# Where the low half of the value weights is made: from GpSimd to VectorE, between the product with the gates and its own low half

## What is computed

```python
def peer(h, w_q, sub_keys, expert_u, expert_v):
    ...
    s_fin, pos = lax.top_k(cand, PEER_TOPK)          # 8 heads x 16 of 16384 experts per token
    ids = jnp.take_along_axis(ids_cand, pos, axis=-1)
    gates = jax.nn.softmax(s_fin, axis=-1)
    ...
        a = jax.nn.gelu(jnp.einsum('cd,ckd->ck', xc, expert_u[idc]))
        return jnp.einsum('ck,ckd->cd', gc * a, expert_v[idc])
```

## Time and profile before

| | us |
|---|---|
| median of 3 runs | 1842.11 (1841.93 to 1848.57) |
| the profiled execution | 1840.62 |
| its span, first to last instruction | 1838.6 |
| TensorE busy in it | 1724.5 (94%) |
| VectorE busy | 1284.1 (70%) |
| GpSimd busy | 1151.2 (63%) |

### The profile page before, as it was taken

How to read it: one execution, slowest core, us unless ns; L and a number is a source line. 1 busy time by engine, 2 the same in 40 slices (tenths; PEclk the granted TensorE clock), 3 DMA queues, 4 the chain that set the end, 5 groups by cost and what they waited for, 6 DMA issues and landing times.

```text
span 1838.6 us, 26701 instructions
## 1 busy us (share of the span) xinstructions
PE 1724.5 (94%) x9077; PEld 1474.0 (80%) x9077; DVE 1284.1 (70%) x2106; ACT 741.6 (40%) x1105; POOL 1151.2 (63%) x701
## 2 busy tenths in 40 slices
PE   6988999999999999998399999999999999999997
PEld 5766778888788999998399999997777777777775
DVE  6678521221221499999999999618888888888887
ACT  5477632322332333332166666533333333333333
POOL 6522224444433468887377777768778888888883
PEclk9999999999999999999699999999999999999999
DMA  6211122222322358787479999989979999999993
GB/s 240 92 46 46 36 69 92 98 96 95 99 69 80 124 167 294 255 258 240 151 245 347 345 344 347 356 334 378 355 301 336 351 356 348 339 345 360 353 343 111
DMA packets 127105, 424.76 MB, mean 231 GB/s; under 512 B 13264, under 2 KB 29648, under 8 KB 124880
## 3 DMA queue, kind: packets, MB, share of 16 engines
q1 hardware_dynamic: 89904, 289.45, 45.3%
q0 software_dynamic: 36864, 134.23, 19.1%
q10 hardware_dynamic: 288, 0.54, 0.1%
HBM read 371.74 MB, written 52.43 MB: 231 GB/s over the span
## 4 chain that ended last, share of the span: by engine, by line
PE 45%; DVE 40%; ACT 6%; issue 5%; DMA 2%; DVEq 1%; SPq 0%; POOL 0%; ACTq 0%
PE both L512 14%; DVE wf L1502 12%; PE bank L523 9%; DVE both L1518 8%; PE bank L512 7%; PE bank L527 5%; DVE rows L1386 4%; ACT wT_hi L1102 3%; PE bank L805 2%; DVE cand L1369 2%; PE bank L722 2%; DVE cand L1426 2%; DVE cand L1423 1%; PE bank L822 1%; DVE topi L1375 1%
## 5 line engine op out<-in xcount | busy, mean ns | idle before, releaser
L466 POOL TENSOR_TENSOR w_lo<-raw,w_hi 128x1024 fp32r<-128x1024 f32 (+1 forms) x430 | 862.8, 2015 | 610.3 <-ACT w_hi L870 608.4
L870 ACT ACTIVATE w_hi<-raw 128x1024 fp32r<-128x1024 f32 x346 | 365.9, 1058 | 599.2 <-PE bank L527 287.5
L523 PE MATMUL bank<-hT_hi,w_hi 128*128 128x384 f32 x1024 | 348.0, 340 | 0.0
L523 PE MATMUL bank<-hT_lo,w_hi 128*128 128x384 f32 x1024 | 343.4, 335 | 0.0
L487 POOL DMA_INDIRECT rows<-stream,idx x256 | 284.8, 1112 | 60.4 <-issue 27.1
L1502 DVE TENSOR_TENSOR wf<-a_in,g_in 128x384 f32<-128x384 f32 x128 | 236.9, 1850 | 27.9 <-DMA a_in<-a_rows 26.3
L822 PE MATMUL bank<-w_hi,wT_hi 128*128 128x512 f32 x768 | 211.6, 410 | 31.1 <-ACT wT_hi L1102 29.6
L822 PEld LDWEIGHTS bank<-w_hi,wT_hi 128*128 128x128 f32 x768 | 134.7, 188 | 105.7 <-ACT wT_hi L1102 79.2
L1102 ACT ACTIVATE wT_hi<-wf 128x384 fp32r<-128x384 f32 x128 | 66.9, 523 | 370.1 <-DVE wf L1502 366.3
L527 PE MATMUL bank<-hT_hi,w_lo 128*128 128x384 f32 x1024 | 199.9, 336 | 6.3 <-POOL w_lo L466 6.3
L822 PE MATMUL bank<-w_hi,wT_lo 128*128 128x512 f32 x768 | 196.6, 391 | 0.0
(11 more groups left out here) (249 smaller groups left out, 2204.0 us busy)
## 6 DMA issues: line engine op xcount, KB each, us to landing
raw<-stream SPq DMA_DIRECT2D x346, 512.0 KB
a_rows<-abuf SPq DMA_DIRECT2D x64, 384.0 KB
g_rows<-gstage SPq DMA_DIRECT2D x32, 768.0 KB
g_in<-g_rows SPq DMA_DIRECT2D x16, 1536.0 KB
a_in<-a_rows SPq DMA_DIRECT2D x64, 384.0 KB
rows<-stream,idx POOLq DMA_INDIRECT x256
x_sb<-x SPq DMA_DIRECT2D x4, 512.0 KB, 8.7
out<-x_sb SPq DMA_DIRECT2D x4, 512.0 KB, 2.6
```

Of the source, the lines that this page charges most:

```text
L466: last = pool.tensor_tensor(w_lo[:, k % 2, cols], raw[:, k % RAW, cols], w_hi[:, k % 2, cols].bitcast(f32), ALU.subtract)
L523: pe.matmul(dst, w_hi[:, slot, k * P:(k + 1) * P], hT[low][:, k, DENSE], start=(k == 0 and low == 0), stop=False)
L870: act.activation(w_hi[:, base % 2, :], raw[:, slot, :], ACT.Copy).then_inc(hi_ready, 1)
```

## The change

In the value stage the low half of the weights is no longer made by GpSimd but by VectorE, as the second of its instructions in a step: after `wf` and ahead of `wT_lo`. It has a semaphore of its own, `value_lo_ready`, on which TensorE and the raw loads of that stage now wait. GpSimd's program in the value stage holds gathers alone, which wait only for a free slot (`dotted`, eight back). The number of matmuls, transfers and bytes stays the same.

```diff
--- before.py
+++ after.py
@@ -238,6 +238,7 @@
 
         raw_loaded = [sem(f"raw_loaded{i}") for i in range(RAW)]
         hi_ready, lo_ready, chunk_used = sem("hi_ready"), sem("lo_ready"), sem("chunk_used")
+        value_lo_ready = sem("value_lo_ready")
         proj_read = sem("proj_read")
         mem_loaded, gains_loaded, small_loaded = sem("mem_loaded"), sem("gains_loaded"), sem("small_loaded")
         x_loaded = [sem(f"x_loaded{t}") for t in range(TT)]
@@ -298,8 +299,10 @@
             a_rows = dram["a"]
             g_rows = dram["g"]
 
-            def load(n, slot, fresh=False):
-                if not fresh:
+            def load(n, slot, fresh=False, value=None):
+                if value is not None:
+                    sp.wait_ge(value_lo_ready, value)
+                elif not fresh:
                     sp.wait_ge(lo_ready, n - RAW + 1)
                 sp.dma_start(raw[:, slot, :], stream[bass.ds(n, 1), :, :].rearrange("n p c -> p (n c)")
                              ).then_inc(raw_loaded[slot], 16)
@@ -385,7 +388,8 @@
 
             for k in range(I_TAIL):
                 at = I_PLAIN + I_GATES + k
-                load(first_u + at, (first_u + at) % RAW)
+                early = first_u + at - RAW + 1 - S_EV
+                load(first_u + at, (first_u + at) % RAW, value=early if early > 0 else None)
                 if k % 2:
                     store_a(0, at // 2)
                 if k == 0:
@@ -409,7 +413,7 @@
 
             def value_step(j0, k, more=True, again=True):
                 if more:
-                    load(j0 * 2 + (nxt + k), (nxt + k) % RAW)
+                    load(j0 * 2 + (nxt + k), (nxt + k) % RAW, value=j0 * 2 + (nxt + k - RAW + 1 - S_EV))
                 if k % 2 and again:
                     reload_a(j0, k // 2 + 4)
 
@@ -490,7 +494,8 @@
 
             g = 0
             for c in range(2 * NI):
-                low(S_U + c, S_U + c)
+                if c < NI:
+                    low(S_U + c, S_U + c)
                 while g < 2 * HK and gather_after(g) <= c:
                     gather(g)
                     g += 1
@@ -833,11 +838,11 @@
                 if not final:
                     for t in range(1, TT):
                         both(t, wT_lo, w_hi)
-                    pe.wait_ge(lo_ready, n + i0 + 1)
+                    pe.wait_ge(value_lo_ready, i0 + (di + 1))
                     for t in range(1, TT):
                         last = both(t, wT_hi, w_lo)
                 else:
-                    pe.wait_ge(lo_ready, n + i0 + 1)
+                    pe.wait_ge(value_lo_ready, i0 + (di + 1))
                     for t in range(1, TT):
                         both(t, wT_lo, w_hi)
                         last = both(t, wT_hi, w_lo, stop=True)
@@ -1502,6 +1507,11 @@
                 dve.tensor_tensor(wf[:, di % 2, :].rearrange(tiles, b=BLOCKS),
                                   a_in[:, di % 8, :].rearrange(tiles, b=BLOCKS),
                                   g_in[:, di // GROUP, :, di % GROUP, :], ALU.mult).then_inc(weighted, 1)
+                dve.wait_ge(hi_ready, i0 + (S_EV + di + 1))
+                if first:
+                    dve.wait_ge(chunk_used, S_EV + di - 1)
+                dve.tensor_tensor(w_lo[:, di % 2, :], raw[:, (S_EV + di) % RAW, :], w_hi[:, di % 2, :].bitcast(f32),
+                                  ALU.subtract).then_inc(value_lo_ready, 1)
                 dve.wait_ge(weighted_hi, i0 + (di + 1))
                 dve.tensor_tensor(wT_lo[:, di % 2, :], wf[:, di % 2, :], wT_hi[:, di % 2, :].bitcast(f32),
                                   ALU.subtract).then_inc(weighted_lo, 1)
```

## The result

The changed kernel takes 1785.95 us (median of 4 runs, 1785.6 to 1787.23), the kernel before 1842.02 beside it (4 runs, 1841.87 to 1848.57). The ratio is 0.9683, 95% interval 0.9664 to 0.9701. The forecast was 1779 in a range of 1771 to 1801: the sign, the mechanism and the range held, and the time is 7 us over the forecast. It lies 1 us above the band of 1772 to 1785 that stood for DMA keeping up, within the band of the DMA rival, though what that rival says did not happen; the account behind the experiments says what lifted it.

What follows compares the result with a forecast made beforehand. VectorE, held up by GpSimd's subtraction, was taken to bound the value stage. Chunk 6 at 1264.7, 121 chunks of 4.08 (493.7), 15.0 behind, 2.0 around, 2 for late loads: 1777.4; median 1.5 higher, 1779 us, range 1771 to 1801.

Steps and rivals of the forecast that it cites:

- DMA keeping up: Value stage: DMA can carry the 388 GB/s that 4.08 us a chunk needs; 1772 to 1785 us, chance 0.62.
- the DMA rival: Value stage: DMA holds today's ratio, 378 GB/s, 4.19 us a chunk, 13 us more, 1792; band 1785 to 1800, chance 0.18.
- The room, 0.526 us a chunk: Value stage: chunks can fall from 4.606 us to TensorE's 4.08, a floor the change cannot pass.
- `wf` shortened by the overlap: VectorE, value stage: without GpSimd subtracting at the same time, `wf` falls from a mean of 1.85 us to about 0.56.
- Price of the subtraction: VectorE, value stage: the moved 1024-column subtraction takes 1.22 us, 1.14 from start to start, between 1.05 and 2.40.
- VectorE's step of 3.75: Value stage: VectorE's work per step after the change, gathered rows included, 3.75 us, under TensorE's 4.08.
- The new wait: VectorE, value stage: `w_lo` waits for ScalarE's `w_hi` in about every third step, at most 1 us; costed at nothing.
- The estimate from the 358 GB/s of the Trainium skill: Value stage: at about 358 GB/s between HBM and SBUF a chunk takes 4.43 us, the sum 42 us higher, 1821.
- the 353: Value stage: DMA rate of the stage's best whole window; as ceiling, 4.49 us a chunk, 50 us more, 1829, chance 0.05.
- The entry: Start of the value stage: DMA backlog lets chunk 6 start between 1262.8 and 1266.6, early gathers delaying it; middle 1264.7 taken.
- late raw loads: After the value stage's entry: some raw loads come late while the DMA backlog goes down; 2 us added.
- Chunk 0 starts at 1237.23 and that stays: Start of the value stage: unchanged at 1237.23 us, as the u stage in front is not touched.

Runs made afterwards that it cites:

- strip: The kernel before, with GpSimd's value-stage subtraction cut to 8 of its 1024 columns and none on VectorE; two executions, 1783.6 and 1778.6 us.
- half_more: The changed kernel, with a further 512-column subtraction by VectorE into a spare tile, and a drain, in each step; 1829.3 us.
- twice: The changed kernel, with VectorE making the full subtraction twice, once into a spare tile with a drain behind it; 1884.4 us.
- behind: The changed kernel, with VectorE's subtraction for `w_lo` placed behind the one for `wT_lo` instead of ahead; 1813.7 and 1815.1 us.
- paced: The changed kernel, with GpSimd's gathers held to their old places by a wait for `value_lo_ready`; 1774.9 to 1785.9 us.
- entry: The changed kernel, with SyncE's wait for all activation stores and the `gfin` load moved behind the first 16 value steps; 1777.6 us.

## Why the prediction came out as it did

- **The room, 0.526 us a chunk, with 4.08 as the floor: right.** 4.607 became 4.082. It was read from four steps of the kernel before in which VectorE had nothing to add.
- **`wf` shortened by the overlap: right.** 1.850 to 0.563 us, and strip shows that it was GpSimd's subtraction.
- **Price of the subtraction, 1.22: right** (1.224), and VectorE's step of 3.75 as well; half_more and twice fall where the sum puts them.
- **The new wait costs nothing: right in the result**, 57 waits of at most 0.6 us, in nearly every second step where every third was forecast. The reason given was too short: it counted TensorE's cover and not that the place fills VectorE's own hole. behind shows what that is worth, 35 us.
- **DMA keeps up at 388 GB/s: right.** 388 was measured, 400 over 100 us, so neither today's ratio (378) nor the 353 was a ceiling. The estimate from the 358 GB/s of the Trainium skill, "SBUF — State Buffer", Summary: rules for kernel authors, 1821, lies 35 us above the measured time. The trace does not contradict the about 425 for a core streaming alone of the Trainium skill, "HBM Reference"; that figure stands under Specifications (TRN2), and not under Access as the prediction has it.
- **The entry: the interval held, the middle not.** Chunk 6 was to start 25.6 to 29.4 us after chunk 0 and did so after 28.65, near the end that stood for early gathers in the way; I had taken the middle, 27.5. Whether it was the gathers is open, with paced for it and strip against. What is shown is that SyncE stands still for 9.7 us, and that the loss goes when it does not (entry). For late raw loads I had added 2 us; 1.5 came, but through the clock.
- **"Chunk 0 starts at 1237.23 and that stays": this is the step that failed**, and the only one that moved the sum. It cost 8.9 us. Without it the sum is right to 1 us: 1246.17 + (1773.4 - 1237.23) = 1782.3, and 2 for the late loads, 1784.3 against a span of 1785.2. I had taken for granted that the same instructions in front take the same time. They do not: the attention stage has two ways to run, which made 7.1 of the 8.9, and 2.3 arose ahead of it with their cause open. The spread of the kernel before, 1841.93 to 1848.57 in three executions, was a sign of it, and I did not ask what it was.
- **That the time is only 7 us off is in part luck.** The profiled execution was forecast at 1777.4 and took 1787.23, 9.8 more. The median was to lie 1.5 above it and lies 1.3 below, which gives 2.8 back. And the range held the time because its top was drawn for a DMA limit, which did not show.

## What to carry to other kernels

When an instruction of one engine holds up those of another that it meets, its cost is also the time that it takes from them; find the steps in which the partner happens to be idle, and read the true price there. A subtraction moved onto the busy engine can be free if it goes into a hole of that engine's own, so look for what that engine waits for, not only for what waits on it. A queue that waits for one thing holds up all that stands behind it: put what is needed at the end at the end. And a stage that a change does not touch may still move: look at the spread of the kernel before and at what makes it, before taking its start for fixed.

## What the runs showed that was not expected

- The same instructions of the attention stage take 13.24 or 14.57 us a head pair, depending on whether GpSimd's subtraction begins near the end of VectorE's normalisations or just behind their start, and from the second head pair on a trace mostly keeps to one way (behind, with a mean of 14.16, is the exception). With one wait on GpSimd the eight normalisations took 2.2 us in each head pair of four traces, and ten executions of the kernel before lay within 3.1 us, against 10.9 without.
- After an idle time of 3.75 us TensorE was granted half its clock for most of 4 us, with a cost of 1.5 us on top of the idle time (0.58 on average from 1275 to 1279). The kernel before, which idled 1.55 us at the same place, kept its full clock there (1.00 from 1266 to 1270).
- The DMA engines of the one core that the program uses carried 400 GB/s for 100 us at a share of 1.00 without anyone waiting for data.
